# Values of four attention units in one stretch of TensorE, with five slots of turned probabilities and paired stores

## What is computed

```python
scores = q @ k.T + bias            # three dilated causal patterns, all inside the causal half
out    = sum over patterns of softmax weights x values
mixed  = concat(deltanet_out, out * silu(gate))
result = x + mixed @ w_out
```

## Time and profile before

| | |
|---|---|
| time of the runs | median 1482.88 us (1482.83 to 1483.05, 3 runs) |
| span of the profiled execution | 1480.8 us; the page gives no other time for that execution, and the median lies 2.1 us above its span |
| TensorE matmuls busy | 97% of the span |
| VectorE / ScalarE / GpSimd busy | 54% / 42% / 29% |
| this stage | from 1250 us to 1382 us of the span, 8 heads |
| granted TensorE clock in it | 1.00 |

### The profile page before, as it was taken

How to read it: one execution, slowest core, us unless ns; L and a number is a source line. 1 busy time by engine, 2 the same in 40 slices (tenths; PEclk the granted TensorE clock), 3 DMA queues, 4 the chain that set the end, 5 groups by cost and what they waited for, 6 DMA issues and landing times.

```text
span 1480.8 us, 30804 instructions
## 1 busy us (share of the span) xinstructions
PE 1438.2 (97%) x12682; PEld 1268.2 (86%) x12682; DVE 801.8 (54%) x1475; ACT 622.0 (42%) x1250; POOL 427.0 (29%) x527
## 2 busy tenths in 40 slices
PE   7999999989999999999999999999998998999998
PEld 7999998867777788888899999888897887888887
DVE  6238310149999878745420723452424776888431
ACT  6323121027777677632432112332335554777210
POOL 0212132110000277622202212221205874434320
PEclk9999999999999999999999999999999999999999
DMA  7313222000000033356325244433121021222342
GB/s 252 65 54 104 97 79 81 16 1 0 1 1 1 19 122 98 80 178 171 93 43 59 50 95 84 61 58 57 29 66 43 27 91 40 67 78 68 100 134 80
DMA packets 88017, 105.32 MB, mean 71 GB/s; under 512 B 25343, under 2 KB 72095, under 8 KB 87880
## 3 DMA queue, kind: packets, MB, share of 16 engines
q1 hardware_dynamic: 87880, 103.36, 26.7%
HBM read 80.20 MB, written 23.12 MB: 70 GB/s over the span
## 4 chain that ended last, share of the span: by engine, by line
PE 57%; DVE 4%; ACT 2%; issue 1%; DMA 1%; POOL 0%; DVEq 0%; SPq 0%; ACTq 0%
PE ps L378 22%; PE ps L1346 12%; PE ps L2851 2%; PE ps L1154 2%; PE ps L1138 2%; PE ps L2837 2%; PE ps L2826 1%; PE ps L2227 1%; PE ps L2170 1%; PE ps L2185 1%; DMA p_w_raw<-w_in 1%; PE ps L1131 1%; PE ps L1133 1%; PE ps L1132 1%; PE ps L2814 1%
## 5 line engine op out<-in xcount | busy, mean ns | idle before, releaser
L344 POOL TENSOR_TENSOR p_w_lo<-p_w_raw,p_w_hi 128x2048 fp32r<-128x2048 f32 (+1 forms) x27 | 127.7, 4728 | 505.7 <-ACT p_w_hi L318 505.7
L378 PE MATMUL ps<-p_w_hi,w_out_hi 128*128 128x256 f32 (+1 forms) x640 | 181.9, 284 | 1.2 <-ACT p_spill L403 1.1
L378 PE MATMUL ps<-p_w_hi,w_out_lo 128*128 128x256 f32 (+1 forms) x640 | 179.7, 281 | 0.0
L378 PE MATMUL ps<-p_w_lo,w_out_hi 128*128 128x256 f32 (+1 forms) x640 | 179.6, 281 | 0.0
L378 PE MATMUL ps<-p_w_hi,hT_hi 128*128 128x256 f32 x576 | 163.7, 284 | 1.5 <-DVE hT_lo L140 1.5
L378 PE MATMUL ps<-p_w_hi,hT_lo 128*128 128x256 f32 x576 | 162.6, 282 | 0.0
L378 PE MATMUL ps<-p_w_lo,hT_hi 128*128 128x256 f32 x576 | 162.6, 282 | 0.0
L378 PEld LDWEIGHTS ps<-p_w_hi,w_out_hi 128*128 128x128 f32 x640 | 120.6, 188 | 2.3 <-ACT p_spill L403 1.6
L378 PEld LDWEIGHTS ps<-p_w_lo,w_out_hi 128*128 128x128 f32 x640 | 120.8, 189 | 0.0
L378 PEld LDWEIGHTS ps<-p_w_hi,w_out_lo 128*128 128x128 f32 x640 | 120.6, 188 | 0.0
L378 PEld LDWEIGHTS ps<-p_w_hi,hT_hi 128*128 128x128 f32 x576 | 109.0, 189 | 1.9 <-DVE hT_lo L140 1.9
(11 more groups left out here) (306 smaller groups left out, 3590.2 us busy)
## 6 DMA issues: line engine op xcount, KB each, us to landing
p_w_raw<-w_in SPq DMA_DIRECT2D x26, 1024.0 KB, 8.0
s_gate<-p_spill SPq DMA_DIRECT2D x48, 128.0 KB, 1.8
kbT<-x SPq DMA_DIRECT2D x8, 512.0 KB, 6.5
b_w_raw<-w_out SPq DMA_DIRECT2D x8, 512.0 KB, 3.4
qT<-s_gate SPq DMA_DIRECT2D x8, 512.0 KB, 6.9
qT<-x SPq DMA_DIRECT2D x8, 512.0 KB, 3.3
s_x<-qT SPq DMA_DIRECT2D x8, 512.0 KB, 3.0
c_table<-s_line SPq DMA_DIRECT2D x8, 512.0 KB, 3.6
```

Source lines behind the costliest of these rows:

```text
L344: ops.tensor_tensor(self.w_lo[:, c % 2, :, 0:w], self.raw[:, :, 0:w], self.w_hi[:, c % 2, :, 0:w].bitcast(F32), ALU.subtract).then_inc(sel ...
L378: last = self.nc.tensor.matmul(out, lhs, rhs, start=(kt == 0 and i == 0), stop=(kt == KT - 1 and i == 2))
```

## The change

- TensorE does the values of four units in one stretch, in the steps u = 4, 8, ..., 60 (units u-4 to u-1), and those of units 60 to 63 behind `out.turn(pe, 0)`. A stretch has 72 matmuls in place of 36.
- Units u and u+2 of a group of four share an output bank: units 0 and 2 lie side by side in bank 6, units 1 and 3 in bank 7.
- A stretch waits until all units of the group before are stored. A store waits until all four units of its group are done.
- VectorE stores two units ahead of `bias_and_max` in the steps u = 4k+1 (units 4k-4, 4k-3) and u = 4k+2 (units 4k-2, 4k-1), and none in the other two. The last four units are stored behind the loop. Near the end the stores stand ahead of `out.mix`.
- The ring of turned probabilities has five slots in place of three.

```diff
+    STEP, RING = 4, 5
...
+    def sums(u, half):
+
+        return ps[half, 6 + u % 2, u % STEP // 2 * HD:u % STEP // 2 * HD + HD]
...
-            if u >= 2:
-                pe.wait_ge(out_stored, u - 1)
+            if u >= STEP:
+                pe.wait_ge(out_stored, u // STEP * STEP)
             for j in range(blocks(u)):
                 for q in range(2):
-                    last = nc.tensor.matmul(ps[q * HD:(q + 1) * HD, 6 + u % 2, 0:HD],
-                                            prob_t[:, u % 3, j * P + q * HD:j * P + (q + 1) * HD],
+                    last = nc.tensor.matmul(sums(u, slice(q * HD, (q + 1) * HD)),
+                                            prob_t[:, u % RING, j * P + q * HD:j * P + (q + 1) * HD],
...
-            if u >= 2 and u % 2 == 0:
-                values(u - 2)
-                values(u - 1)
-        values(n_units - 2)
+            if u and u % STEP == 0:
+                for n in range(u - STEP, u):
+                    values(n)
         pe.wait_ge(max_ready, n_units)
         out.turn(pe, 0)
-        values(n_units - 1)
+        for n in range(n_units - STEP, n_units):
+            values(n)
...
-                    if u >= 3:
-                        dve.wait_ge(out_ready, u - 2)
-                    nc.vector.tensor_copy(prob_t[:, u % 3, first * P:end * P],
+                    if u >= RING:
+                        dve.wait_ge(out_ready, u - RING + 1)
+                    nc.vector.tensor_copy(prob_t[:, u % RING, first * P:end * P],
...
-            dve.wait_ge(out_ready, u + 1)
-            nc.vector.tensor_scalar(g.att_tok[:, i, h * HD:(h + 1) * HD], ps[:, 6 + u % 2, 0:HD], stat[:, 2, u:u + 1],
+            dve.wait_ge(out_ready, u // STEP * STEP + STEP)
+            nc.vector.tensor_scalar(g.att_tok[:, i, h * HD:(h + 1) * HD], sums(u, slice(0, P)), stat[:, 2, u:u + 1],
...
+            if u >= STEP and u % STEP in (1, 2):
+                for n in (2 * (u % STEP) - 2, 2 * (u % STEP) - 1):
+                    store(u // STEP * STEP - STEP + n)
             if u == n_units - 3:
                 out.mix(dve, 0)
             if u == n_units - 1:
                 out.mix(dve, 1)
-            if u >= 3:
-                store(u - 3)
             if u + 2 < n_units:
                 bias_and_max(u + 2)
             empty(u)
...
-        for u in range(n_units - 3, n_units):
+        for u in range(n_units - STEP, n_units):
             store(u)
...
-                    if u >= 3:
-                        act.wait_ge(out_ready, u - 2)
-                    nc.scalar.copy(prob_t[:, u % 3, first * P:end * P],
+                    if u >= RING:
+                        act.wait_ge(out_ready, u - RING + 1)
+                    nc.scalar.copy(prob_t[:, u % RING, first * P:end * P],
...
-        g.c_prob_t = k.sb("c_prob_t", [P, 3, SEQ])
+        g.c_prob_t = k.sb("c_prob_t", [P, 5, SEQ])
```

## The result

The change makes the kernel slower: 1499.13 us (1498.89 to 1499.54, 4 runs) against 1482.97 us (1482.83 to 1483.52, 4 runs), a ratio of 1.0107 with a 95% interval of 1.0095 to 1.0119. The profiled execution has a span of 1497.2 us, against 1480.8: +16.4.

A forecast was written before the change was run, and what follows sets the result against it. TensorE was taken to bound the kernel before, a loop through three engines the one after. Head 0 -0.35, six heads +11.2 and the end +3.2 give +14.0: span 1494.8, plus 2.1 to the median, 1496.9 us; range 1488 to 1501.

The forecast's parts named there:

- a loop through three engines: Per head, u0's bias to u4's and back through TensorE, VectorE and ScalarE: 9.24 + 8.68 = 17.92 us, against 16.0.
- Rival A: TensorE stays the bound in the stage, so only fixed costs go: faster, 1478.2 us; chance 0.09.
- Rival B: Only the first half of a head is bound by the loop: +0.5 us a head, 1488.8 us; chance 0.09.
- The signs: In the profile after: heads of 17.9 us, stretches of about 2.3, TensorE waits of 0.3 to 0.8, VectorE idle about 1.
- The fixed cost of a stretch: Each TensorE value stretch pays a fixed 0.35 us; 17 fewer stretches save 5.9 us of its work.
- the old loop: Same two sums with the old terms: 7.79 + 7.47 = 15.26 us a head, under the 16.0 measured.
- The end: From unit 56's turning to the projection: +1.6 and +1.7, together +3.2 us, at least 1.2, at most about 4.2.
- exponentials of 512 columns and signal 0.95, turning 0.43: Terms between unit 63's scores and the projection, in a sum of 9.5 us against 7.76 before.
- The clock: TensorE's granted clock falls to the lower level as it idles some 3 us in 18: over 1505 us; chance 0.03.
- head 0: First head loses its first stretch (-1.40) and its second grows by 1.05: -0.35 us, between -1.40 and +1.05.

The follow-up runs named there:

- the doubled scores: TensorE forms the scores of units u1 and u5 twice: 1487.52 us in the kernel before, 1497.5 us in the kernel after.
- the stores out: Changed kernel with units 4k and 4k+1 sharing a bank, stored while the other two are multiplied, the other pair in step 4k+1: 1491.03 us.
- even preps: Preps of the next head moved to the even steps: 1491.38 us in the kernel after, 1480.91 us in the kernel before.
- all three: Changed kernel with stores out of the loop, preps in even steps and the last group in twos: 1486.2 us.
- the four runs behind it: On all three: stretch ahead of turning, 1491.57; plus exponentials first in steps 4k, 1489.29; plus u4's prep ahead, 1489.3. All three with u4/u0 exponentials first: 1500.01 us.
- its old end: Changed kernel with the last group of four handled as in the kernel before, each unit stored when done: 1495.79 us.

## Why the prediction was right, step by step

**The bound.** The forecast's mechanism is a loop through three engines that is longer than TensorE's own work. That TensorE's work no longer sets the time is shown by the doubled scores: +0.58 us a head before, nothing after. That the stores are in the loop is shown by the run that took them out: heads of 16.91 us, 16.8 expected. Rival A would have had TensorE still busy 19.8 of 20 us; it is busy 17.82. Rival B would have added about 0.5 us to a head; it is 1.83.

**The signs.** Heads of 17.9, the stretches of 2.3 us, VectorE's idle 0.8 to 0.95 us ahead of the first scaling and the four scalings in a row ahead of L1377 all came. TensorE's waits came in part only. I named the scores of u4 and u0; the wait for a bias stands ahead of u6's scores alone (0.54), and its counterpart in the other half is missing. Ahead of the turnings of u0 and u4 TensorE idles no more than 0.1 us, but both start 0.05 us behind the end of ScalarE's exponentials (1341.13 to 1341.18, 1350.14 to 1350.19), so these do release them, as the sum has it. The wait ahead of u7's turning (0.49, for ScalarE's copy) I did not foresee; it is not among the terms of the loop.

**The loop's terms.** In the rows above, from u0's bias done (1338.62 + 1.22 = 1339.84): 1.34 to the turning (1.40 forecast), 3.71 to u3's scores (3.65), 1.71 to the low part, 0.72 to the next instruction, 0.80 for two stores, 0.95 for the bias: 9.23 us, forecast 9.24. From there: 2.41 to u4's prep (0.04 + 0.97 + 0.62 + 0.83 = 2.46), 2.81 to u7's scores (2.81), 0.78 to its bias, 1.39 to u0's bias (1.42), 1.22: 8.61, forecast 8.68. A head of 17.83 for 17.92, and six of them +10.6 for +11.2, where head 1's smaller start (1269.92 to 1287.68, 17.76) is in. Here the differences of starts carried over almost to the hundredth. They did so for a change that kept nearly every queue as it was. For the orders further off the same kind of sum did worse: 16.8 expected and 16.91 measured with the stores out, 16.2 and 16.4 to 16.6 with even preps, but 15.5 to 15.7 and 16.37 with all three, 15.1 to 15.4 and 16.80, 16.0 to 16.2 and 16.57, 15.6 to 15.9 and 16.32, 16.2 to 16.4 and 18.5 in the four runs behind it, always too low.

**The fixed cost of a stretch.** From a prep to the second score matmul it is 1342.11 to 1345.11 = 3.00 us with 72 value matmuls between: 1.95 + 1.05, so the second 36 cost 0.029 each and no second fixed 0.35. The rule of the Trainium skill that stood beside it (TensorEngine Tiling (Array Packing), Key Properties: a change of the tiling mode drains TensorE) is in agreement with that, though no run here separates a drain from other costs of the change between 128x128 and 128x64 work. The saving is real, but it falls into TensorE's waits.

**The slack before the change was overstated.** I had 15.26 us for the old loop against a head of 16.0, and took the 0.7 between for slack under TensorE's own work. The run of even preps in the kernel before has heads of 15.62 with the same work: TensorE's own work is at most that, and 0.34 of the 16.0 was a wait, of which the row showed 0.18. The slack against TensorE's work was some 0.36. It did not change the forecast, since the new loop lies over 2 us above either.

**The end was sized too low**: +4.2 for +3.2. From unit 56's turning to unit 63's scores it is 10.41 us (10.2 forecast). From those scores to the projection it is 10.24 where I had 9.5 (before 7.76). The step that was sized wrong is "exponentials of 512 columns and signal 0.95, turning 0.43": I had unit 63's turning wait for its exponentials alone. They end at 1390.30, but its bank had to be emptied of unit 62's first piece, and ScalarE's copy of that piece (1390.21, 0.56) stood behind the exponentials; the turning, after 1.71 us of idle time, began at 1390.91, 0.61 us behind the exponentials. These 0.61 are most of the 0.74 by which the part was too low. It is within the bound given for the end (4.2), for another reason than the one named there.

**The clock** was a rival of its own, for a fall in every head, with over 1505 us. In the heads it never came. It came once in the stage and the projection, behind the longest wait, and took 1.8 us, which no term of the sum held. With it the difference between the forecast 1496.9 and the 1499.13 measured is accounted for: +1.8 for the clock, +1.0 for the end, +0.24 ahead of the stage, -0.6 for heads 1 to 6 and -0.15 for head 0 are 2.3 us. The errors in the heads and at the end nearly cancel, which is luck; the mechanism does not hang on it, since each is small against the 10.6 us of heads 1 to 6.

## What to carry to other kernels

Before an order is changed to save work on the busiest engine, follow one result around the loop through the other engines and back, as a sum of differences of starts, and compare that sum with the busy engine's own work: here the longer stretch added 1.05 us to each half of the loop and saved TensorE 0.35. On engines that take their work in order, moving one instruction ahead delays all that is queued behind the others; both rearrangements here that put exponentials first removed the wait that they aimed at, and each made another (0.39 us became 1.25 in the second). Before a profile's longer head is put down to a wait, its granted clock has to be looked at: u4's prep ahead of its stretch gained 0.25 us a head, and a fall of the clock hid it. And a small wait on an engine that is "97% busy" can be the better target: moving the preps in the kernel before took 0.37 us from each head and made the only faster version.

## What the hardware showed that was not expected

TensorE's granted clock fell to its lower level behind a wait of 1.80 us at the end of the stage and was back after some 3.4 us (1.7 us lost at half speed): 1.00, then 0.76, 0.50, 0.89 in windows of 2 us, with the matmuls of 512 columns 0.43 us apart in place of 0.23. In the same window of 2 us, the one in which that wait ends (1396 to 1398), TensorE was busy 0.51 us there and 0.39 us in the kernel after with doubled scores, which had the same wait of 1.80 and kept 1.00. In the profile of the kernel after with even preps the fall came behind the wait of 1.71 us ahead of unit 63's turning and not behind the one of 1.80 ahead of the projection, and with u4's prep first it came in head 0, behind a wait of 1.75. In the kernel after with its old end there was none in the projection. All these profiles, that of the kernel before too, also show a fall ahead of the stage, between 1122 and 1132 us, of a length that differs from profile to profile. Whether a fall comes is therefore not settled by the wait's length or by how busy TensorE was in that window, and what settles it stays open. In the kernel after it was worth up to 1.8 us, a ninth of the effect studied.
